# Sums over channels of the branch norms: two fp32r products with a rounded matrix of ones in place of one native fp32 matmul

## The reference

```python
def rmsnorm(x, w):
    xf = x.astype(jnp.float32)
    y = xf * lax.rsqrt(jnp.mean(xf * xf, axis=-1, keepdims=True) + EPS)
    return (y * w.astype(jnp.float32)).astype(x.dtype)

# in mixer_layer, SSD branch: 2 groups of 512 channels
y = y.reshape(bsz, l, SSD_GROUPS, gw) * silu(z).reshape(bsz, l, SSD_GROUPS, gw)
y_ssd = rmsnorm(y, ssd_norm_w.reshape(SSD_GROUPS, gw)).reshape(bsz, l, D_SSD)
# retention branch: 8 heads of 64 channels
y_ret = rmsnorm(o, ret_norm_w.reshape(RET_HEADS, RET_HEAD_DIM)).reshape(bsz, l, D_RET) * silu(g_ret)
mix = concatenate([y_ssd, y_ret, y_pool], axis=-1)
x = x + mix @ w_out
```

## Time and profile before

| | |
|---|---|
| median of 3 runs | 966.02 us |
| the profiled execution's own time | 961.38 us |
| its span, first to last instruction | 959.6 us |
| TensorE busy | 940.4 us (98%) |
| VectorE busy | 693.5 us (72%) |
| ScalarE busy | 417.0 us (43%) |
| mean granted clock of TensorE | 0.997 |

### The profile page before, as it was taken

One profiled execution on the slowest core, in us unless ns is written; L12 is line 12 of the kernel. 1 busy time (PEld: TensorE's weight loads), 2 busy tenths in 40 slices (PEclk: granted clock), 3 DMA queues, 4 the chain that ended last, 5 costly groups with the idle time before them and its releaser, 6 DMA issues.

```text
span 959.6 us, 18795 instructions
## 1 busy us (share of the span) xinstructions
PE 940.4 (98%) x7950; PEld 893.8 (93%) x7950; DVE 693.5 (72%) x946; ACT 417.0 (43%) x699; POOL 43.7 (5%) x148
## 2 busy tenths in 40 slices
PE   8999999999999999999999999999999999999996
PEld 7899999999989889999999999999989988899995
DVE  6789777866996568664557987788679757686445
ACT  5432464234774135532334235533277633544222
POOL 0000011010010000000000001011101000000000
PEclk9999999999999999999999999999999999999998
DMA  7234221234244453323332352222423452552322
GB/s 276 92 109 151 75 67 53 66 111 155 88 108 156 152 217 121 137 95 109 133 129 66 113 152 58 66 67 61 166 89 120 137 194 56 224 201 66 89 67 99
DMA packets 38277, 112.56 MB, mean 117 GB/s; under 512 B 11088, under 2 KB 14032, under 8 KB 36784
## 3 DMA queue, kind: packets, MB, share of 16 engines
q1 hardware_dynamic: 37936, 110.46, 34.9%
q0 software_dynamic: 256, 0.88, 0.3%
HBM read 93.85 MB, written 17.47 MB: 116 GB/s over the span
## 4 chain that ended last, share of the span: by engine, by line
PE 78%; DVE 14%; ACT 5%; issue 1%; DMA 1%; SPq 0%; DVEq 0%; ACTq 0%
PE acc L546 22%; PE acc L548 21%; PE acc L547 21%; DVE w_lo L1199 3%; PE misc L678 1%; ACT decay L1021 1%; ACT w_hi L930 1%; DVE conv_out L1325 1%; DVE qk L1330 1%; DVE conv_out L1327 1%; PE misc L664 1%; PE misc L731 1%; DVE qk L1328 1%; PE misc L753 1%; PE acc L821 1%
## 5 line engine op out<-in xcount | busy, mean ns | idle before, releaser
L546 PE MATMUL acc<-hin,w_hi 128*128 128x288 f32 x1504 | 450.9, 300 | 3.4 <-DVE w_lo L1199 3.4
L548 PE MATMUL acc<-hin,w_lo 128*128 128x288 f32 x1504 | 442.9, 294 | 0.0
L547 PE MATMUL acc<-hin,w_hi 128*128 128x288 f32 x1504 | 442.9, 294 | 0.0
L546 PEld LDWEIGHTS acc<-hin,w_hi 128*128 128x128 f32 x1504 | 282.1, 188 | 16.5 <-issue 10.8
L930 ACT ACTIVATE w_hi<-w_raw 128x1024 fp32r<-128x1024 f32 x120 | 126.8, 1057 | 374.5 <-PE acc L548 372.1
L547 PEld LDWEIGHTS acc<-hin,w_hi 128*128 128x128 f32 x1504 | 282.2, 188 | 0.4
L548 PEld LDWEIGHTS acc<-hin,w_lo 128*128 128x128 f32 x1504 | 282.1, 188 | 0.0
L1199 DVE TENSOR_TENSOR w_lo<-w_raw,w_hi 128x1024 fp32r<-128x1024 f32 x120 | 146.4, 1220 | 121.0 <-ACT w_hi L930 120.8
L546 PE MATMUL acc<-mix,w_hi 128*128 128x288 f32 x416 | 124.3, 299 | 2.7 <-DVE mix L1205 1.3
L548 PE MATMUL acc<-mix,w_lo 128*128 128x288 f32 x416 | 122.6, 295 | 0.0
L547 PE MATMUL acc<-mix,w_hi 128*128 128x288 f32 x416 | 122.5, 294 | 0.0
(11 more groups left out here) (218 smaller groups left out, 1056.6 us busy)
## 6 DMA issues: line engine op xcount, KB each, us to landing
w_raw<-in_w SPq DMA_DIRECT2D x120, 512.0 KB, 3.6
decay<-cum_rows SPq DMA_DIRECT2D x8, 1024.0 KB, 6.8
h<-in_ssm SPq DMA_DIRECT2D x16, 512.0 KB, 6.1
out_ssm_s<-h SPq DMA_DIRECT2D x16, 512.0 KB, 6.2
x<-in_x SPq DMA_DIRECT2D x8, 576.0 KB, 6.3
x_kept<-x SPq DMA_DIRECT2D x4, 576.0 KB, 2.8
x<-x_kept SPq DMA_DIRECT2D x4, 576.0 KB, 5.9
out_y<-x SPq DMA_DIRECT2D x8, 288.0 KB, 2.2
```

The lines of the kernel that those rows point to most:

```text
L546: pe.matmul(out, wh, hi, start=k == 0, stop=False)
L547: pe.matmul(out, wh, lo, start=False, stop=False)
L548: return pe.matmul(out, wl, hi, start=False, stop=k == KT - 1)
```

## The change

The squares of each norm are no longer multiplied natively. ScalarE copies them, rounded to fp32r (`sq_hi`, signalled by `b_hi`); VectorE subtracts the copy from the squares (`low`, giving `sq_lo` and the signal `b_lo`); TensorE multiplies both with a matrix of ones, rounded to fp32r once a layer (`sums_r`), and adds the products in PSUM. Ones are exact in fp32r. TensorE waits for `b_lo` where it waited for `b_sq` or `b_add`. The diff without the placing of the new tiles in memory (they lie over dead ones) and the two new semaphores:

```diff
@@ -793,23 +806,27 @@
 
             def ret_norm_sum(i):
 
-                pe.wait_ge(*of(b_sq, i + 1))
+                pe.wait_ge(*of(b_lo, i + 1))
                 if i == 0:
                     pe.wait_ge(*of(hs_n, 4))
                 if i >= 2:
                     pe.wait_ge(*of(b_ln, i - 1))
                 for half in range(2):
-                    mm = pe.matmul(mb[:, 2 * (i % 2) + half, 0:HALF], blk, halves(ret_sq[i])[:, half, :],
-                                   start=True, stop=True)
+                    out = mb[:, 2 * (i % 2) + half, 0:HALF]
+                    pe.matmul(out, sums_r[:, 1, :], halves(sq_hi[i])[:, half, :], start=True, stop=False)
+                    mm = pe.matmul(out, sums_r[:, 1, :], halves(sq_lo[i])[:, half, :],
+                                   start=False, stop=True)
                 mm.then_inc(b_sum, 1)
 
             def ssd_norm_sum(g):
 
-                pe.wait_ge(*of(b_add, 4 * (g + 1)))
+                pe.wait_ge(*of(b_lo, RP + g + 1))
                 pe.wait_ge(*of(b_ln, RP))
                 for half in range(2):
-                    mm = pe.matmul(mb[:, 2 * g + half, 0:HALF], ones, halves(z_gate[g])[:, half, :],
-                                   start=True, stop=True)
+                    out = mb[:, 2 * g + half, 0:HALF]
+                    pe.matmul(out, sums_r[:, 0, :], halves(sq_hi[RP + g])[:, half, :], start=True, stop=False)
+                    mm = pe.matmul(out, sums_r[:, 0, :], halves(sq_lo[RP + g])[:, half, :],
+                                   start=False, stop=True)
                 mm.then_inc(b_sum, 1)
 
             def pool_mm_(g):
@@ -1141,9 +1158,14 @@
                         eng.wait_ge(*of(pool_out, 4))
                         for i in range(RP):
                             go(act(ret_sq[i], qk[:, i, :], ACT.Square), b_sq, i + 1)
+                        settle()
+                        for i in range(2):
+                            go(act(sq_hi[i], ret_sq[i], ACT.Copy), b_hi, i + 1)
                     if u == S_RN + 1:
                         eng.preload_act_table_set("natural_log_exp_and_others")
                         two_rstd(0, HD)
+                        for i in range(2, RP):
+                            go(act(sq_hi[i], ret_sq[i], ACT.Copy), b_hi, i + 1)
                         two_rstd(2, HD)
                     if u == S_RL:
                         for i in range(RP):
@@ -1158,6 +1180,8 @@
                             else:
                                 eng.wait_ge(*of(b_add, j - 1))
                             go(act(tmp[:, j % 2, :], xbc[:, j, :], ACT.Square), b_sq, RP + j + 1)
+                        eng.wait_ge(*of(b_add, 4 * g + 4))
+                        go(act(sq_hi[RP + g], z_gate[g], ACT.Copy), b_hi, RP + g + 1)
                     if u == S_NORM + GROUPS:
                         eng.preload_act_table_set("natural_log_exp_and_others")
                         two_rstd(RP, PAIRS // GROUPS * P)
@@ -1603,6 +1627,12 @@
                                           op1=ALU.mult), b_used, i + 1)
                 settle()
                 go(V.tensor_tensor(q, q, qk[:, RP + i, :], ALU.mult), ret_full, i + 1)
+
+            def low(i, square):
+
+                eng.wait_ge(*of(b_hi, i + 1))
+                settle()
+                go(V.tensor_tensor(sq_lo[i], square, sq_hi[i].bitcast(F32), ALU.subtract), b_lo, i + 1)
 
             def mix_low(which, i):
 
@@ -1701,6 +1731,12 @@
 
                     for i in {S_GATE: (0, 1), S_GATE + 1: (2, 3), S_RL + 1: (4, 5, 6, 7)}.get(u, ()):
                         z_use(i)
+                    if u == S_RN:
+                        go(V.tensor_copy(sums_r[:, 0, :], ones))
+                        go(V.tensor_copy(sums_r[:, 1, :], blk))
+                    if u in (S_RN, S_RN + 1):
+                        for i in (2 * (u - S_RN), 2 * (u - S_RN) + 1):
+                            low(i, ret_sq[i])
                     if u in (S_RN + 1, S_RN + 2):
                         for i in (2 * (u - S_RN - 1), 2 * (u - S_RN - 1) + 1):
                             ret_out(i)
@@ -1721,6 +1757,7 @@
                                 go(V.tensor_copy(z_gate[g], tmp[:, j % 2, :]), b_add, j + 1)
                             else:
                                 go(V.tensor_tensor(z_gate[g], z_gate[g], tmp[:, j % 2, :], ALU.add), b_add, j + 1)
+                        low(RP + g, z_gate[g])
                     if S_NORM + GROUPS <= u < S_NORM + GROUPS + 4:
                         for j in (2 * (u - S_NORM - GROUPS), 2 * (u - S_NORM - GROUPS) + 1):
                             y = xbc[:, j, :]
```

More of the change, by code:

```diff
@@ L179, in trunk @@
         rS = place("ret_state", [P, RP, P], at=rw + 4 * 4096)
+        xbc_at = top[0]
         xbc_two = place("xbc", [P, CONV_CHUNKS, TOK + SMP])
@@ L185, in trunk @@
         vT = place("vT", [P, RP, TOK])
+        halo_at = top[0]
         halo = place("halo", [P, 2, PHALO])
+        cvt_at = top[0]
         cvt = place("conv_out", [P, 2, PHALO])
+        tmp_at = top[0]
         tmp = place("tmp", [P, 2, TOK])
@@ L217, in trunk @@
         rstds = (rstd[:, :], ssq[:, :])
+        row = 4 * (TOK + SMP)
+        high_of = [place(f"branch_square_high_{i}", [P, TOK], F32R, at=xbc_at + row * (8 + i))[:, :] for i in range(4)]
+        sq_hi = [high_of[2 + i % 2] for i in range(RP)] + high_of[0:GROUPS]
+        sq_lo = [place(f"branch_square_low_{i}", [P, TOK], F32R, at=at)[:, :]
+                 for i, at in enumerate((tmp_at, tmp_at + 4 * TOK, xbc_at + row * 8, xbc_at + row * 9,
+                                         halo_at, cvt_at))]
         z_gate = [halo[:, 0, 0:TOK], halo[:, 1, 0:TOK], cvt[:, 0, 0:TOK], cvt[:, 1, 0:TOK]]
@@ L222, in trunk @@
         vtok = place("v_tok", [P, RP * P])
+        sums_r = place("sum_matrices_rounded", [P, 2, P], F32R, at=vtok_at)
         cpad = place("c_padded", [P, GROUPS, NB, 32], at=vtok_at)
@@ L348, in trunk @@
         b_sq = sem("branch_squared", RP + PAIRS)
+        b_hi = sem("branch_squares_high", RP + GROUPS)
+        b_lo = sem("branch_squares_split", RP + GROUPS)
         b_add = sem("branch_squares_added", PAIRS)
```

## The result

The changed kernel takes 986.67 us (median of 4 runs, 985.1 to 988.8) against 965.86 us before. The ratio is 1.022, 95% interval 1.020 to 1.024: 2.2% slower. The forecast was 981.3, the range 976.5 to 988.0.

A forecast was written before the change was run, and what follows sets the result against it. TensorE, busy 98% of the span, was taken to bound the kernel. The profiled 961.4 us plus 7.65 us a layer (15.3) gave 976.7; with 4.6 from profile to median, 981.3 us. Range 976.5 to 988.

The forecast's parts named there:

- the likeliest case: Whole kernel: waits at three places a layer add 15.3 us, clock stays full: 981.3 us; chance 0.55.
- rival A: TensorE's clock also falls in the waits, about 1.5 us a time: 984.3 to 988.4 us; chance 0.33.
- Place 1: Unit 39, VectorE: state additions stand behind subtractions awaiting ScalarE's copies; TensorE starts 3.9 us later a layer.
- Place 2: Unit 41: copies behind ScalarE's exponentials delay VectorE's subtractions and split(43); unit 43 is 2.8 us late a layer.
- Place 3: Units 44 to 46: extra copy delays group 1; TensorE waits 1.8 us before the last sum, 0.95 lost a layer.
- The sum: Place 1, Place 2 and Place 3 together: 3.9 + 2.8 + 0.95 = 7.65 us a layer, 15.3 us for both.
- a clock below 1.00 in the middle: Sign against the forecast: TensorE's granted clock dipping below 1.00 in the middle of the changed trace.
- B: VectorE's subtractions are hidden and only TensorE's saving of 5.2 us counts: 960.8 us, faster; chance 0.04.
- C: Place 1 costs 3.9 us, later places nothing, as earlier-fed logarithms let ScalarE run ahead: 968.6 us; chance 0.05.
- D: TensorE's fp32r products cost 0.48 us each, like the native call, so it gains nothing: 984.1 us; chance 0.03.
- the most that the change can gain: TensorE, 24 norm-sum calls: two fp32r products take 0.27 us where a native call takes 0.48, 5.2 us in all.
- The offset: Whole kernel: the median of the runs stands 4.6 us above the profiled execution; added to the forecast.

The follow-up runs named there:

- e1_place1: Changed kernel with the two casts and subtractions 0 and 1 moved between the third and fourth group of state additions: 973.61 us, ratio 1.007.
- native_waits: Changed kernel with its copies, subtractions and waits, but each sum one native fp32 product of the high part: 986.71 us, ratio 1.022.
- fills: Changed kernel with TensorE's three waits a layer filled with 32, 22 and 12 fp32r products that no result needs: 981.59 us, ratio 1.015.
- before_again: The kernel before, unchanged, run for a second profile: 967.27 us.
- e2_place2: Changed kernel with ScalarE's copies 2 and 3 moved ahead of the read of z and the logarithms: 981.44 us, ratio 1.016.
- e3_place3: Changed kernel with the last sum moved from behind unit 46 into unit 47, after product 7: 982.66 us, ratio 1.016.
- gain_only: Changed kernel with squares written rounded to fp32r and multiplied twice, without copies, subtractions or added waits: 963.17 us, ratio 0.997.
- e123_all: Changed kernel with the edits of e1_place1, e2_place2 and e3_place3 together, all added instructions kept: 963.76 us, ratio 0.997.

## Why the prediction was right, and where it was not

The time lies inside the range, near its upper end. The three places cost nearly what the working said; the clock, which the likeliest case kept at full, did not stay there, and rival A came true.

**Place 1** was forecast at 3.9 us a layer. From 348.14 to 349.05 before, from the same L561 at 347.82 to 352.68 after: 0.91 and 4.86, so 3.95. The chain behind it, squares, copies, two subtractions and then the additions, is the one seen above. e1_place1 shows that it is the place and not the work.

**Place 2** was forecast at 2.8. From the first sum to unit 43: 16.60 us before, 19.47 after (358.60 to 378.07), so 2.87, and the wait for `w_lo` of 0.68 is in it as said. The saving of the four sums is hidden in it: in native_waits, without it, the wait at sum 2 is shorter by the same 0.86 us (2.32 against 3.18).

**Place 3** was forecast at 0.95. From unit 43 to the second matmul after the last sum: 27.64 us before (370.03 to 397.67), 28.89 after (378.07 to 406.96), so 1.25. This term was too small by 0.3. Group 0's additions end as reckoned (397.52: the 389.49 of before plus the 8.04 us by which unit 43 is late), but ScalarE's high(47) starts after the copy has ended, where the working let it start 0.10 us before that:

```profile
397.56 0.69 ACT L1184 ACTIVATE branch_square_high<-halo 128x576 fp32r<-128x576 f32 x1 [0.98 <-DVE halo L1759]
398.29 1.06 ACT L947 ACTIVATE w_hi<-w_raw 128x1024 fp32r<-128x1024 f32 x1
```

So group 1 is 0.76 us late and not 0.6. The rest is that the first product behind the wait takes 0.24 us to the next start (406.19 to 406.43) and not 0.13.

**The sum** of 7.65 us a layer was 8.07 in the first layer of the profile, and fills, with the clock at full in the norms, gives 15.7 us for both layers against 15.3.

**The clock** is the step of the likeliest case that failed. That case let it stay at full, and named a clock below 1.00 in the middle as a sign against itself; rival A, at 0.33, had it fall and gave 984.3 to 988.4, and that is what happened: 986.7. Its price was reckoned at 1.5 us a time from the kernel's own start. In the profile the stretch from L728 to the first sum is 5.92 us in the first layer and 6.54 in the second, against 4.38, so 1.5 and 2.2. That the first of these is the reckoned figure is luck in part: the windows at the start have a granted clock of 1.00, so that what made their products slow was the clock isn't shown. fills shows the whole of it, 5 us by the medians. TensorE's busy time was expected to fall by 5 us and rose by 5.2, for the same reason: matmuls at half clock are busy for longer (before_again has 946.7 us of them and the first profile 940.4, for the same work). What spoke for the rival was underrated: the only row on the clock, the end of the trace, had it fall 2 us after the last matmul, and the waits forecast were longer.
The Trainium skill's rule on waits between groups of matmuls (TensorE: Matmul & The Clock Gate, section HAM oscillation — how this bites in real kernels) agrees with these traces in part. In the profiles of the changed kernel, e1_place1, e2_place2, e3_place3 and native_waits all eight waits of 4.57 us at place 1 come with a slow stretch, and three of the four of 3.2 us at place 2. Of their twelve waits of 1.3 to 2.8 us at places 2 and 3 only one does (1.88 us, first layer of the changed kernel). So the prediction's reading, that by this rule every stall is paid with a slow stretch, does not hold here.

**Rivals.** B is out: the subtractions were not hidden. C too: place 2 costs its 2.87 us in full behind place 1, and e1_place1 leaves it with a wait of 2.8. D is out by the starts of L816 and L817, 0.13 us apart. What the prediction called the most that the change can gain, 5.2 us, can't be had either: gain_only and e123_all end 2 to 4 us below before, because the saving of sums 0 to 3 runs into VectorE, which was just in time at unit 43 already. The prediction had seen that both arrive together there, and did not draw this from it.

**The offset** of 4.6 us from profile to median was carried along unexplained. before_again explains it by two slow stretches in unit 22. No run shows that the changed kernel's median holds the same 4.6: its profile has one short stretch there, worth 1.5 us, and its median stands 1.6 above that profile. So the time is near to the forecast partly by luck. The waits of the two profiles differ by nearly 16 us and the slow clock of the norms adds 6.4, together more than the 20.8 between the medians, because in the changed kernel's profile the slow clock in unit 22 costs less than in before's median.

## What to carry to other kernels

Where one engine is busy 98% of the time, ask of each added instruction not how long it is but what stands behind it in its queue and who awaits that. Three edits of order, with no work taken away, turned 2.2% slower into 0.3% faster. A saving on the busiest engine counts only as far as the next engine's work is early; where both arrive together, it is worth next to nothing (0.36 of 1.74 us here). To learn what the clock costs behind a wait, fill the wait with products that no result needs and compare the times. Take a second profile before trusting an offset between the profiled execution and the median.

## What the runs showed of the hardware

- In the changed kernel's profile TensorE waited 4.57, 3.18 and 1.88 us, and during or behind some of these waits the granted clock was 0.50 (353.0 to 356.5, 407.7 to 411.1, 830.9 to 837.7, 848.0 to 854.8). Starts of fp32r products of 288 columns were 0.24 us apart in place of 0.133. In fills, with products in the waits, the clock stayed at 1.00 in the norms of both layers.
- The clock also falls with TensorE never idle: in a block of 128 native 64x8 instructions, with TensorE busy 1.00 in the windows before and behind the fall (before_again, from 186.7 us). Mean clocks of the executions of before reach from 0.991 to 0.997, and their times from 967.8 to 961.2 us in step with it, a spread of 0.7%.
- Two 128x128 casts from fp32 to fp32r on VectorE start 0.14 us apart, recorded at 0.22 each.
